# The first norm's token factor applied to the in-projection's sums in PSUM, with x loaded and begun in two token halves

## The chip, the cores and the metric

The kernel runs on one core of a Trainium2 chip. The metric is the device time of one execution in microseconds (us). TensorE (PE) does the matmuls, VectorE (DVE), ScalarE (ACT) and GpSimd (POOL) the rest; SyncE (SP) issues most transfers. The profile names weight loads of TensorE apart (PEld).

## The reference, cut to what matters

The program is a recurrent block followed by a second block. Only the front of the first block meets the change: a norm over the 1024 channels of each of 1024 tokens, the in-projection, and then two branches, a gated recurrence (LRU) and a short convolution (SC).

```python
def rms_norm(x, g):
    xf = x.astype(jnp.float32)
    y = xf * lax.rsqrt(jnp.mean(xf * xf, axis=-1, keepdims=True) + EPS)
    return (y * g.astype(jnp.float32)).astype(x.dtype)
...
        h = rms_norm(x, norm1_g[l])
        z = jnp.einsum('bsd,de->bse', h, w_in[l])
        lru_x, lru_gate, sc_b, sc_c, sc_x = jnp.split(z, splits, axis=-1)
        lru_x = causal_dwconv(lru_x, lru_conv_w[l]) + lru_conv_b[l]
        y_lru = rg_lru(lru_x, lru_wa[l], lru_ba[l], lru_wx[l], lru_bx[l], lru_lambda[l]) \
            * jax.nn.gelu(lru_gate)
        y_sc = sc_b * causal_dwconv(sc_c * sc_x, sc_conv_w[l])
```

The norm is x times a gain per channel times a factor per token. The factor per token can be taken out of the sum over channels, so z can be had as (x times gain) times w_in, times the factor.

## The kernel before

All data is fp32. Activations are held with channels on the 128 partitions and the 1024 tokens along the free axis, so x, which arrives with tokens on partitions (`x_tok`, 4 transfers of 1 MB), is transposed on TensorE: 8 token tiles of 8 transposes each, copied from PSUM into `xs`. A product of full precision is made of three matmuls in fp32r: both operands are split into a rounded part (`_hi`, a cast on ScalarE) and the rest (`_lo`, a subtraction: for weights on GpSimd, for `h` half on VectorE, half on GpSimd). `matmul3` issues the three, each in two halves of 512 tokens; `project` does that for the 8 channel tiles, 48 matmuls for one block of 128 outputs and all 1024 tokens, and then raises `block_done`.

The order on every engine is written out by hand; engines meet at semaphores. There are four PSUM tiles `ps[0]` to `ps[3]` of 1024 columns.

Start (`L603` to `L656`, `L1067` to `L1089`, `L1609` to `L1666`, `L2279` to `L2340`): x is loaded and transposed; VectorE squares 7 token tiles, ScalarE one; the root and its reciprocal give `rstd`, which 8 small matmuls (16 records, L2279) spread over the partitions into `ps[2]`. VectorE then forms h = xs times gain times factor for each channel tile (L1609) into `scr`, ScalarE casts it (L1061), VectorE and GpSimd make the rests (L1621, L958), and `first_two` multiplies the first two blocks, X(0) and G(0), channel tile by channel tile as they come. While TensorE is at that, ScalarE takes one Exp (L1089) and VectorE works out the gates' constants from it in a chain of small steps (L1649 to L1666). The first convolution (`conv_first`, L1098) waits for those constants, for `x_parked` (a 4 MB copy of `xs` to HBM, since the convolution overwrites `xs`) and for X(0).

The recurrence goes over 8 channel tiles c. TensorE's order in it is X(c), the gates of tile c-1 (12 matmuls), G(c). X(c) may begin when `conv_done` says that the convolution of X(c-1) has left `ps[0]`; the gates of c-1 wait for `xc_lo_done`; G(c) waits for `gelu_done` of c-1, which reads `ps[1]`. ScalarE's order is `conv_first(c)`, the cast of the next weights, five curves of tile c-1 (`gate_curves`, with two table loads), a cast of the gate weights, then `gate_gelu(c)`: cast of weights, cast of `xc`, GELU of G(c). VectorE's order is the three taps of the convolution (`convolve(c)`, L1625), `recur(c-1)` (L1680 to L1694, nine steps and among them a scan), `second_parts(c)` (L1698, L1701), and again from the start.

Then come 12 blocks for the SC branch, S(0) to S(11), where ScalarE copies the C part out of PSUM (`sc_c`, L1258), VectorE multiplies it with the X part (L1805), convolves, and multiplies with the B part (L1810). From L2352 on follow the out-projection, the feed-forward part and the second block, which the change doesn't touch but for numbers of a semaphore.

## Time and profile before

| | |
|---|---|
| three runs | 1728.16, 1730.13 and 1732.98 us, median 1730.13 us |
| profiled execution | span of 1726.5 us from the first to the last instruction; no other time of it is on record |
| median of the runs less that span | 3.6 us |
| TensorE matmul busy | 1681.0 us (97%) |
| VectorE busy | 1225.3 us (71%) |
| ScalarE busy | 792.4 us (46%) |
| GpSimd busy | 516.6 us (30%) |
| mean granted TensorE clock | 0.992 of full speed |

The shares are means over stages with different limits. The 3.6 us lie around the span (launch and end). Times in the rows below count from the first instruction of the profiled execution.

### The profile page before, as it was taken

The numbers are of one execution on the slowest core, as the hardware profiler recorded it, in microseconds if no ns is written. First come the engines' busy times: TensorE is split into PE (matmuls) and PEld (weight loads), VectorE is DVE, ScalarE is ACT, GpSimd is POOL, SyncE is SP. The second block draws the span as 40 slices with busy tenths as digits, with TensorE's granted clock in tenths as the row PEclk, the third lists the DMA queues.
The fourth block names the chain that finished last, engine by engine and source line by source line (L and its number), as shares of the span: only waits on it lengthen the run. The fifth ranks groups of instructions, "written<-read, shape, count | busy, mean of one in ns | idle before, by whom it ended". The sixth has DMA issues, their size and how long they took to land.

```text
span 1726.5 us, 20915 instructions
## 1 busy us (share of the span) xinstructions
PE 1681.0 (97%) x7556; PEld 1383.3 (80%) x7556; DVE 1225.3 (71%) x1442; ACT 792.4 (46%) x1038; POOL 516.6 (30%) x284
## 2 busy tenths in 40 slices
PE   7999999999999999999999999998999999999998
PEld 6888878888877888888888888886878877777776
DVE  6577772259999888888888789885636365666554
ACT  5466541235764434343434455553322146676531
POOL 4221222200015555554552000003432242345320
PEclk8999999999999999999999999999999999999999
DMA  8111112152422232222223876651321320110251
GB/s 259 49 36 49 40 45 74 37 201 80 152 81 76 83 97 73 84 84 87 73 86 125 317 237 199 219 159 43 122 74 61 85 86 25 37 49 25 102 215 73
DMA packets 161095, 176.96 MB, mean 102 GB/s; under 512 B 13566, under 2 KB 114692, under 8 KB 161028
## 3 DMA queue, kind: packets, MB, share of 16 engines
q1 hardware_dynamic: 158724, 167.67, 30.3%
q10 hardware_dynamic: 2304, 8.39, 1.3%
q8 instruction: 42, 0.69, 0.2%
q14 instruction: 25, 0.20, 0.0%
HBM read 140.38 MB, written 35.65 MB: 102 GB/s over the span
## 4 chain that ended last, share of the span: by engine, by line
PE 82%; DVE 10%; ACT 4%; issue 1%; POOL 1%; DMA 1%; POOLq 0%; DVEq 0%; ACTq 0%; SPq 0%
PE ps L921 28%; PE ps L2398 24%; PE ps L2352 18%; PE ps L2618 4%; PE ps L2603 3%; PE ps L2648 2%; PE ps L2588 1%; DVE lat L2109 1%; PE ps L2576 1%; DVE pt_lo L2203 1%; DVE prob L2185 1%; POOL z_lo L1015 1%; PE ps L2279 1%; DVE square_dve L1636 0%; ACT pt_hi L1548 0%
## 5 line engine op out<-in xcount | busy, mean ns | idle before, releaser
L945 POOL TENSOR_TENSOR w_lo<-w_raw,w_hi 128x1024 fp32r<-128x1024 f32 x52 | 135.8, 2614 | 623.0 <-ACT w_hi L1044 623.0
L2398 PE MATMUL ps<-hop_hi_P,wop_hi_P 128*128 128x512 f32 x672 | 262.5, 391 | 4.7 <-DVE u L1853 3.3
L2398 PE MATMUL ps<-hop_hi_P,wop_lo_P 128*128 128x512 f32 x672 | 261.5, 389 | 0.0
L2398 PE MATMUL ps<-hop_lo_P,wop_hi_P 128*128 128x512 f32 x672 | 261.5, 389 | 0.0
L921 PE MATMUL ps<-h_hi,w_hi 128*128 128x512 f32 x752 | 235.1, 394 | 11.3 <-DVE h_lo L1621 7.8
L951 POOL TENSOR_TENSOR wop_lo_P<-pair_sum,wop_hi_P 128x512 fp32r<-128x512 f32 x90 | 135.9, 1510 | 354.5 <-ACT wop_hi_P L1055 354.5
L921 PE MATMUL ps<-h_lo,w_hi 128*128 128x512 f32 x752 | 232.9, 391 | 0.0
L921 PE MATMUL ps<-h_hi,w_lo 128*128 128x512 f32 x752 | 232.7, 391 | 0.0
L921 PEld LDWEIGHTS ps<-h_hi,w_hi 128*128 128x128 f32 x752 | 141.4, 189 | 43.3 <-issue 14.0
L921 PEld LDWEIGHTS ps<-h_lo,w_hi 128*128 128x128 f32 x752 | 142.1, 189 | 29.8
L921 PEld LDWEIGHTS ps<-h_hi,w_lo 128*128 128x128 f32 x752 | 142.0, 189 | 29.7
L2398 PEld LDWEIGHTS ps<-hop_hi_P,wop_hi_P 128*128 128x128 f32 x672 | 126.1, 188 | 33.7 <-DVE u L1853 4.5
L2398 PEld LDWEIGHTS ps<-hop_hi_P,wop_lo_P 128*128 128x128 f32 x672 | 126.1, 188 | 26.3
L2398 PEld LDWEIGHTS ps<-hop_lo_P,wop_hi_P 128*128 128x128 f32 x672 | 126.1, 188 | 25.8
L2352 PE MATMUL ps<-dn_x_hi,dn_w_hi 128*128 128x512 f32 x336 | 131.0, 390 | 0.4 <-DVE dn_x_lo L1735 0.4
L2352 PE MATMUL ps<-dn_x_lo,dn_w_hi 128*128 128x512 f32 x336 | 130.7, 389 | 0.0
L2352 PE MATMUL ps<-dn_x_hi,dn_w_lo 128*128 128x512 f32 x336 | 130.7, 389 | 0.0
L1044 ACT CAST w_hi<-w_raw 128x1024 fp32r<-128x1024 f32 x52 | 54.3, 1048 | 130.6 <-PE ps L921 130.0
L1055 ACT CAST wop_hi_P<-pair_sum 128x512 fp32r<-128x512 f32 x96 | 58.8, 614 | 114.9 <-DVE pair_sum L1842 114.8
L951 POOL TENSOR_TENSOR wop_lo_P<-pair_raw,wop_hi_P 128x512 fp32r<-128x512 f32 x67 | 98.5, 1479 | 2.4 <-ACT wop_hi_P L1055 2.2
L1022 POOL TENSOR_SCALAR mask<-pos_f,vec 128x1024 f32<-128x1024 f32 x16 | 67.4, 4211 | 86.3 <-DVE stat L2185 78.1
L2352 PEld LDWEIGHTS ps<-dn_x_hi,dn_w_hi 128*128 128x128 f32 x336 | 63.1, 188 | 14.4 <-DVE dn_x_lo L1735 1.2
(350 smaller groups left out, 3337.9 us busy)
## 6 DMA issues: line engine op xcount, KB each, us to landing
pair_raw<-in_w_up SPq DMA_DIRECT2D x48, 512.0 KB, 4.6
w_raw<-in_w_in SPq DMA_DIRECT2D x46, 512.0 KB, 3.9
dn_raw<-gu_park SPq DMA_DIRECT2D x84, 256.0 KB, 3.9
dn_raw<-in_w_down SPq DMA_DIRECT2D x60, 256.0 KB, 3.1
gu_park<-up_cv SPq DMA_DIRECT2D x24, 512.0 KB, 2.6
out_raw<-in_w_out SPq DMA_DIRECT2D x30, 256.0 KB, 3.0
x_tok<-in_x SPq DMA_DIRECT2D x4, 1024.0 KB, 8.2
x_park<-xs SPq DMA_DIRECT2D x1, 4096.0 KB, 14.3
```

What stands on the lines that cost most here:

```text
L921: mm = nc.tensor.matmul(out_ap[:, t], w, x[:, t], start=a, stop=b)
L945: nc.gpsimd.tensor_tensor(lo[:, :], raw[:, :], hi[:, :].bitcast(f32), ALU.subtract).then_inc(w_lo_done, 1)
L951: nc.gpsimd.tensor_tensor(wop_lo[q][:, :, :], weight_part(q, pair), wop_hi[q][:, :, :].bitcast(f32), ALU.subtract).then_inc(wop_lo_done, 1)
L1015: nc.gpsimd.tensor_tensor(z_lo[e][:, k, :], raw, z_hi[e][:, k, :].bitcast(f32), ALU.subtract).then_inc(zp_lo_done, 1)
L1022: nc.gpsimd.tensor_scalar(mask[1][:, :], pos_f[:, :], vec[:, V_POS + u % NT:V_POS + u % NT + 1], MASKED, ALU.is_gt, ALU.mult).then_inc(mas ...
L1044: nc.scalar.copy(hi[:, :], raw[:, :]).then_inc(w_hi_done, 1)
L1055: nc.scalar.copy(wop_hi[q][:, :, :], weight_part(q, pair)).then_inc(wop_hi_done, 1)
L2352: mm = nc.tensor.matmul(dst, a[:, w], x[:, :], start=first, stop=last, skip_group_check=True)
L2398: mm = nc.tensor.matmul(dst, w[q][:, k, :], x[q][:, k, :], start=a, stop=b, skip_group_check=True)
L2603: mm = nc.tensor.matmul(dst, a[:, k, d], b[:, k, :], start=first, stop=last)
L2618: mm = nc.tensor.matmul(ps[t % 4][:, c], a[e][:, k, cols_t], b[e][:, k, c], start=first, stop=last)
L2648: mm = nc.tensor.transpose(ps[2][:, k * P:(k + 1) * P], prob[w % 3][:, k * P:(k + 1) * P], ident[:, :])
```

## The change

1. Loads. The 16 small row loads (norm gains, convolution weights, constants, positions) go from SP's queue to ScalarE's, at the head of ScalarE's program. SP issues x in the order x0, x1, weights of X(0), x2, weights of G(0), x3.
2. The front in two token halves T1 and T2 (512 tokens each). The copies of the transposes out of PSUM are divided between ScalarE (even tiles) and VectorE (odd). h without the token factor is made per channel tile and half: its rounded part by one ACTIVATE with the gain as scale (`first_high`), its rest by one VectorE instruction (`first_low`). GpSimd makes no rest of h in the first norm. TensorE does X(0) and G(0) on T1 with the transposes of tokens 4 to 7 set among them, then on T2, with the spreading of the factor in it.
3. The factor. ScalarE copies the spread factor from PSUM to `rstd1` in SBUF. VectorE multiplies each X(c) and each G(c) in place in PSUM with it (`by_token_factor`), before `conv_first` and before the GELU. In the SC branch VectorE takes over the C part, multiplied with the factor squared, and multiplies the convolved product with the factor once more.
4. `gelu_gate`, `square_dve` and `rstd1` get other places in SBUF.

```diff
-            def norm(i, gain, dst, rb, lo_before):
+            def by_token_factor(n, c, bank, done):
+                dve.wait_ge(block_done, read(n, c))
+                V.tensor_tensor(bank[:, :], bank[:, :], rstd1[:, :], ALU.mult).then_inc(done, 1)
...
             def convolve(c, one):
                 xc = xs[:, one, :].rearrange("p o t -> p (o t)")
+                by_token_factor(N_LRU, c, ps[0], zx_done)
                 dve.wait_ge(conv_base, c + 1)
...
+            dve.wait_ge(rstd1_spread, 1)
             convolve(0, first)
             second_parts(0, first)
+            by_token_factor(N_LRU + 1, 0, ps[1], zg_done)
             with step.of(11).loop(LRU_TILES - 2) as i:
                 c = i + 1
                 convolve(c, bass.ds(c, 1))
                 recur(i, bass.ds(i, 1))
                 second_parts(c, bass.ds(c, 1))
+                by_token_factor(N_LRU + 1, c, ps[1], zg_done)
             c = LRU_TILES - 1
             convolve(c, last)
             second_parts(c, last)
             recur(c - 1, slice(c - 1, c))
+            by_token_factor(N_LRU + 1, c, ps[1], zg_done)
             recur(c, last)
...
             def conv_first(c, one):
-                act.wait_ge(block_done, read(N_LRU, c))
+                act.wait_ge(zx_done, c + 1)
...
+                act.wait_ge(zg_done, c + 1)
                 gelu = gelu_last if one is last else gelu_gate
```

ScalarE's new order at the start:

```diff
+            xt_copy(0)
+            xt_copy(2)
+            act.wait_ge(vec_t, 1)
+            nc.scalar.copy(vec[:, :], ps[0][:, 0:V_COLS]).then_inc(vec_done, 1)
+            high(0)
...
+            first_high(0, T1)
+            first_high(1, T1)
+            high(1)
+            first_high(2, T1)
+            first_high(3, T1)
+            xt_copy(4)
+            for c in range(4, KT):
+                first_high(c, T1)
+            xt_copy(6)
...
+            for n in range(5, NT):
...
+                token_square(n)
...
+            for c in range(4):
+                first_high(c, T2)
...
+            for c in range(4, KT):
+                first_high(c, T2)
+            act.wait_ge(rb_done, 1)
+            nc.scalar.copy(rstd1[:, :], ps[2][:, :]).then_inc(rstd1_spread, 1)
             act.wait_ge(setup_done, LAM_ABS)
             nc.scalar.activation(small[:, 24:32], small[:, 16:24], ACT.Exp).then_inc(vec_done, 1)
```

VectorE's, and TensorE's:

```diff
+            def first_low(c, t):
+                dve.wait_ge(first_hi, (0 if t is T1 else KT) + c + 1)
+                V.scalar_tensor_tensor(out=h_lo[:, c, t], in0=xs[:, c, t], scalar=col(V_NORM1 + c),
+                                       in1=h_hi[:, c, t].bitcast(f32), op0=ALU.mult, op1=ALU.subtract
+                                       ).then_inc(first_lo, 1)
...
+            xt_copy(3)
+            token_square(2)
+            dve.wait_ge(vec_done, VEC)
+            first_low(0, T1)
+            first_low(1, T1)
+            xt_copy(5)
+            first_low(2, T1)
+            token_square(3)
+            first_low(3, T1)
+            first_low(4, T1)
+            xt_copy(7)
+            first_low(5, T1)
+            token_square(4)
+            first_low(6, T1)
+            first_low(7, T1)
...
+            transposed(4)
+            transposed(5)
+            for k in range(8 + 3):
+                for b, j in ((0, k), (1, k - 3)):
+                    if 0 <= j < 8:
...
+                        first_step(b, j, T1)
+                if k in (3, 4):
+                    transposed(k + 3)
+            for b in range(2):
+                for k in range(8):
+                    first_step(b, k, T2)
+                    if b == 0 and k == 3:
+                        pe.wait_ge(rstd_done, 1)
+                        pe.wait_ge(xt_by_act, 4)
+                        spread(ps[2]).then_inc(rb_done, 1)
```

And in the SC branch:

```diff
-                nc.scalar.copy(scr[0][:, :], ps[n % 4][:, :]).then_inc(sc_c, 1)
+                V.tensor_tensor(scr[0][:, :], ps[n % 4][:, :], rstd1_squared[:, :], ALU.mult).then_inc(sc_c, 1)
...
                 step(tap(scr[2], scr[1], 2, V_SCW + j))
+                step(V.tensor_tensor(scr[2][:, :], scr[2][:, :], rstd1[:, :], ALU.mult))
```

## Rows read from the trace of the kernel before

**Rows 1.** The chain that ended last: start us, us, what.

```profile
26.82 182.38 PE ps L921 x792
...
248.76 109.08 PE ps L921 x480
```

**Rows 2.** Timeline of the start: start us, us, engine, line, what.

```profile
5.96 9.79 PE L2292 MATMUL ps<-ident,x_tok 128*128 128x128 f32 x64 [5.96 <-DMA x_tok<-in_x]
...
11.35 3.79 ACT L1067 COPY xs<-ps 128x1024 f32<-128x1024 f32 x4 [0.69 <-PE ps L2292]
...
19.05 3.78 PE L2279 MATMUL ps<-ident,rstd 128*128 128x128 f32 x16
...
20.92 4.67 POOL L945 TENSOR_TENSOR w_lo<-w_raw,w_hi 128x1024 fp32r<-128x1024 f32 x2 [17.00 <-ACT w_hi L1044]
...
37.23 1.28 ACT L1089 ACT_TABLE_LOAD   x1
...
39.74 0.21 ACT L1089 ACTIVATE small<-small 128x8 f32<-128x8 f32 x1 [1.23 <-DVE half_ba L1651]
...
42.92 0.17 DVE L1666 TENSOR_SCALAR kx<-kh 128x8 f32<-128x8 f32 x1
```

**Rows 3.** Busy time by stretch: PE, PEld, DVE, ACT, POOL; granted clock, DMA share, GB/s.

```profile
11.30:15.80 4.50, 4.46 (x41) 4.22 (x39) 3.55 (x6) 4.45 (x5) 0.00 (x0) 1.00 1.09 288
18.20:22.90 4.70, 4.57 (x20) 4.14 (x20) 0.00 (x0) 3.58 (x5) 1.98 (x1) 0.50 1.06 268
26.80:31.70 4.90, 4.88 (x12) 3.83 (x13) 4.90 (x5) 2.37 (x3) 3.64 (x2) 0.50 1.02 364
31.70:51.00 19.30, 19.30 (x86) 15.80 (x84) 14.62 (x28) 7.89 (x9) 8.11 (x4) 1.00 0.21 58
```

**Rows 4.** Timeline of TensorE where X(1) begins.

```profile
51.15 0.72 PE L921 MATMUL ps<-h_hi,w_hi 128*128 128x512 f32 x2
```

**Rows 5.** Timeline of VectorE and ScalarE over one turn of the loop.

```profile
108.89 1.23 DVE L1701 TENSOR_TENSOR xc_lo<-xs,xc_hi 128x1024 fp32r<-128x1024 f32 x1
...
111.52 1.21 ACT L1098 ACTIVATE xs<-ps,vec 128x1024 f32 x1 [2.04 <-PE ps L921]
...
113.00 1.28 DVE L1625 SCALAR_TENSOR_TENSOR xs<-ps,vec,xs 128x1023 f32 x1 [2.88 <-ACT xs L1098]
...
119.40 0.69 DVE L1680 TENSOR_SCALAR scr<-scr 128x1024 f32<-128x1024 f32 x1 [2.17 <-ACT scr L1118]
...
127.27 4.37 DVE L1692 TENSOR_TENSOR_SCAN xs<-scr,root 128x1024 f32 x1
...
133.38 1.22 DVE L1701 TENSOR_TENSOR xc_lo<-xs,xc_hi 128x1024 fp32r<-128x1024 f32 x1
...
136.00 1.21 ACT L1098 ACTIVATE xs<-ps,vec 128x1024 f32 x1 [2.04 <-PE ps L921]
```

**Rows 6.** Timeline of GpSimd in that turn.

```profile
113.74 2.41 POOL L945 TENSOR_TENSOR w_lo<-w_raw,w_hi 128x1024 fp32r<-128x1024 f32 x1 [8.73 <-ACT w_hi L1044]
126.11 3.39 POOL L945 TENSOR_TENSOR w_lo<-w_raw,w_hi 128x1024 fp32r<-128x1024 f32 x1 [9.96 <-ACT w_hi L1044]
```

**Rows 7.** Groups by line and form: count, busy us, mean ns, idle before.

```profile
L1928 DVE TENSOR_TENSOR ps<-ps,xs 128x1024 f32<-128x1024 f32 x48 | 59.2, 1232 | 1.6
L1237 ACT ACTIVATE xs<-x_early,vec 128x512 f32<-128x512 f32 x8 | 5.3, 714 | 2.3 <-DVE x_early L1786 2.3
L2069 DVE COPY scr<-ps 128x1024 f32<-128x1024 f32 x4 | 4.9, 1224 | 28.2 <-PE ps L921 28.2
L1735 DVE TENSOR_TENSOR out_x_lo<-xs,out_x_hi 128x512 fp32r<-128x512 f32 x34 | 23.5, 692 | 0.0
L1692 DVE TENSOR_TENSOR_SCAN xs<-scr,root 128x1024 f32<-128x1024 f32 x2 | 4.6, 2292 | 0.1
```

**Rows 8.** Waits of TensorE, 209 to 360 us: total, times, longest.

```profile
PE ps L921 <- POOL w_lo L945: 1.5, 1, 1.5
```

**Rows 9.** DMA issues: KB, median us to landing.

```profile
x_park<-xs SPq DMA_DIRECT2D x1, 4096.0 KB, 14.3
```

More of the change, by code:

```diff
@@ L203, in program @@
         root = tile("root", G0, 14)
-        gelu_gate = tile("gelu_gate", G0, 15)
+        gelu_gate = tile("gelu_gate", G0, 0)
+        rstd1 = tile("rstd1", G0, 15)
         gelu_last = tile("gelu_last", G0, 8)
-        square_dve = tile("square_dve", G0, 15)
+        square_dve = tile("square_dve", G0, 14)
         pair_raw = [at("pair_raw0", G0 + 8 * TILE, [2, KT, P]), at("pair_raw1", W0, [2, KT, P])]
@@ L1064, in xt_copy @@
             def xt_copy(t):
                 act.wait_ge(xt_done, t + 1)
-                nc.scalar.copy(xs[:, :, t * P:(t + 1) * P], ps[t % 3][:, :].rearrange("p (c q) -> p c q", c=KT)
-                               ).then_inc(xt_copied, 1)
-            for t in range(NT - 2):
-                xt_copy(t)
-            act.wait_ge(x_in[3], 16)
-            nc.scalar.activation(scr[4][:, :], x_tok[:, NT - 1, :], ACT.Square,
-                                 accum_out=small[:, NT - 1:NT]).then_inc(sumsq, 1)
@@ L1076, in _, with first_high, token_square @@
-            act.wait_ge(sumsq, 1)
-            act.wait_ge(sumsq_dve, NT - 1)
+                nc.scalar.copy(xs[:, :, t * P:(t + 1) * P], ps[TOKEN_BANK[t]][:, :].rearrange("p (c q) -> p c q", c=KT)
+                               ).then_inc(xt_by_act, 1)
+            def first_high(c, t):
+                nc.scalar.activation(h_hi[:, c, t], xs[:, c, t], ACT.Identity, scale=col(V_NORM1 + c)).then_inc(first_hi, 1)
+            def token_square(n):
+                nc.scalar.activation(scr[4][:, :], x_tok[:, n, :], ACT.Square,
+                                     accum_out=small[:, n:n + 1]).then_inc(sumsq, 1)
@@ L1630, in _, with token_square @@
                 V.memset(sign[32 * q:32 * q + 32, :], -1.0 if q % 2 == 0 else 1.0).then_inc(setup_done, 1)
-            for n in range(NT - 1):
-                if n % 2 == 0:
-                    dve.wait_ge(x_in[n // 2], 16)
+            def token_square(n):
+                dve.wait_ge(x_in[n // 2], 16)
                 if n >= 1:
@@ L1863, in part_of, with wop_low @@
                 return token_part(name, h)
-            def first_low(q, n):
+            def wop_low(q, n):
                 dve.wait_ge(wop_hi_done, nth(q, Pair(0, n)))
@@ L1902, in _ @@
             half_squares(2)
-            first_low("P2", 1)
+            wop_low("P2", 1)
             half_squares(3)
@@ L1907, in _ @@
             hop_low("P6")
-            first_low("P6", 0)
+            wop_low("P6", 0)
             dve.wait_ge(root_done, 2)
@@ L1912, in _ @@
             hop_low("P7")
-            first_low("P5", 1)
+            wop_low("P5", 1)
             dve.wait_ge(x1_parked[1], 16)
-            first_low("P7", 0)
+            wop_low("P7", 0)
             second_sum(Pair(0, 0))
@@ L1918, in _ @@
             hop_low("P3")
-            first_low("P6", 1)
+            wop_low("P6", 1)
             hop_low("P4")
-            first_low("P4", 0)
+            wop_low("P4", 0)
             def scale(pair, name):
@@ L1973, in period @@
                 if the(k, 0):
-                    first_low("P3", 0)
+                    wop_low("P3", 0)
                     pair_sums(Pair(0, 1), (2, 3))
@@ L2316, in first_two, with first_step @@
                             mm.then_inc(block_done, 1)
-            pe.wait_ge(xt_copied, NT)
-            first_two(0, (ps[0], ps[1]), 0)
+            def first_step(b, k, t):
+                pe.wait_ge(first_lo, (0 if t is T1 else KT) + k + 1)
+                wh, wl = blocked(b)
+                for w, x, first, last in ((wh, h_hi, k == 0, False), (wh, h_lo, False, False), (wl, h_hi, False, k == 7)):
+                    mm = nc.tensor.matmul(ps[b][:, t], w[:, k, :], x[:, k, t], start=first, stop=last)
+                if k == 7 and t is T2:
+                    mm.then_inc(block_done, 1)
+            transposed(4)
[3 more added lines that the diff above has]
+                    if 0 <= j < 8:
+                        if j == 0:
+                            pe.wait_ge(w_lo_done, b + 1)
+                        if j == 0 and b == 0:
+                            pe.wait_ge(vec_done, VEC)
+                        if j == 0 and b == 1:
+                            pe.wait_ge(xt_by_dve, 1)
+                        first_step(b, j, T1)
[8 more added lines that the diff above has]
+                        spread(ps[2]).then_inc(rb_done, 1)
             def gates():
```

176 lines of the change are left out of this document (94 added, 82 removed).

## The prediction

> **What bounds the kernel now.** The shares of busy time say TensorE (97%), but the change touches the first 360 us only, so I read that stretch. The chain of waits comes first: from 26.82 us TensorE's matmuls are the chain without a break, up to the recurrence's end, and again from 248.76 [rows 1]. Ahead of 26.82 stands a front in which TensorE does only transposes (5.96 to 15.75) and the spread [rows 2]. So a microsecond saved before 26.82 is a microsecond saved, if nothing later gives it back. Two more views decide whether something does. The stretches by granted clock: after the transposes TensorE runs at 0.50 (1.2 GHz) up to 31.7 us, then at full clock [rows 3]. And one turn of the recurrence's loop on the other engines [rows 5]: the turn is 136.00 - 111.52 = 24.48 us, which is TensorE's 108 matmuls. Is there a second loop just below it? From the start of `conv_first` (111.52) to the first step of `recur` (119.40) are 7.88 us, in which VectorE depends on ScalarE's curves; from there to the end of the `xc_lo` subtraction (133.38 + 1.22 = 134.60) 15.20 us more. VectorE and ScalarE together need 23.08 us for a turn in which each step waits for the one before; only 1.40 us are free, although VectorE's busy share doesn't show it. That is the number on which the prediction rests.
>
> **The change, part by part: the loop.** It puts two multiplies in place in PSUM on VectorE into each turn. The same form (PSUM tile of 1024 columns by an SBUF tile, back into PSUM) takes 1.232 us in this kernel [rows 7], no more and no less to be expected; with some 0.07 for each handover, 2.6 us in all. The one on X(c) stands ahead of `conv_first`, so ScalarE's curves and `recur` move back by it; the one on G(c) stands between `xc_lo` and the next turn's first instruction, and ScalarE's GELU behind it. Neither lies beside a wait. The turn of VectorE and ScalarE becomes 23.08 + 2.6 = 25.7 us, against TensorE's 24.48: TensorE waits 1.2 us a turn, for `xc_lo_done`. Of the turns the first costs 0.4 (it uses up the 1.40 that are free, and its `recur` starts without one before it), the next five 1.2 each: 6.4 us.
>
> That turn holds one stall already: the scan takes 4.37 us in the loop and 2.29 outside it, while GpSimd makes the rest of the next weights (126.11, 3.39 us); GpSimd's other one, at 113.74, takes 2.41 and lies beside VectorE's taps, which read PSUM and don't stretch (1.28) [rows 5, 6, 7]. So two streams from SBUF on VectorE and a GpSimd subtraction exclude each other, and one with an operand in PSUM doesn't take part. The multiplies have one operand in PSUM and stay out of it; the stall stays at one a turn.
>
> **The recurrence's end.** VectorE: taps of tile 7, `second_parts`, `recur(6)`, multiply of G(7), `recur(7)`. The GELU of G(7), which had run under `recur(6)`, now comes after it, and ScalarE's last curves behind the GELU. Then come the casts of the weights of S(2), for whose rest TensorE already waits 1.5 us [rows 8]. To that chain are added 1.3 (X multiply), 1.3 (G multiply), 1.0 (GELU, of the size of a 1024-column copy, 3.79 / 4 = 0.95 [rows 2]), and taken from it 0.9 (the copy of the C part, now VectorE's): 2.7 us. It also starts late by the 1.2 us for which the multiply of X(7) queues behind that of G(6). S(2) comes 3.9 us later against X(7): as two waits, S(1) for the GELU and S(2) for its weights. It is 3 us if GpSimd's stalls fall better here, 5 if worse; I take 3.6, since part of TensorE's wait lies under the loop's own. Loop and end: 10 us, from 8 to 12.
>
> **The SC branch.** VectorE gets three more operations for each j and ScalarE one less. A group of three blocks takes TensorE 33 us and VectorE's steps for it are some 10; `sc_c` of j = 0 comes after `recur(7)`, but S(4), which waits for it, begins two blocks (22 us) after S(2). I cost it at nothing; cover gone, it would be 1.2 us once.
>
> **The start.** What the change takes away is real: no multiply by the factor before the first matmul, no wait for all of x. Tokens 0 to 3 are transposed by about 12.1 us (64 transposes in 9.79, the first at half the pace [rows 2]), the small rows' transposes come at about 13, `vec` 13.3, the cast of the first weights (1.0) 14.3, GpSimd's rest of them (4.67 / 2 = 2.3) 16.7, `first_low(0)` 17.8 with the exclusion above: it reads `xs` and `h_hi` from SBUF and has to wait for GpSimd. First matmul at 17.8, 9.0 us before that of [rows 1]. But from there the halves are fed by long queues:
>
> - T1. `first_low(1)` meets GpSimd's second rest, 20.8. TensorE's matmuls run at 1.2 GHz (0.43 us each in 26.80:31.70, 0.227 at full clock [rows 3]), since the clock fell after the transposes here and nothing else precedes them there. VectorE does a copy (1.22), a square, lows of 0.69 [rows 7]; its copy of token tile 7 waits for the transposes of that tile, which TensorE makes only after step k = 4, at half clock: k = 3 for both blocks 24.6 to 27.3, tile 6 to 28.6, k = 4 to 30.6, tile 7 to 31.6. `first_low(5)` stands behind the copy: 33.5. The last five steps end at 40.4.
> - T2. 48 matmuls of 0.227 = 10.9 and the spread, half of 3.78 at full clock: 53.2. X(0) is complete at 47.7.
> - The chain behind it. The spread ends at 45.0 and only then does ScalarE copy `rstd1` (1.0), load the Exp table (1.28) and take the Exp (0.21); before, table and Exp were done at 39.95, under the first matmuls. VectorE's chain of constants from there takes 42.92 + 0.17 - 39.95 = 3.1 us [rows 2]: 50.6. The multiply of X(0) stands in VectorE's queue behind it (1.3), then `conv_first` (1.2) and three taps (113.00 to 117.2, 4.2) before X(1) may begin: 57.4, against 51.15 [rows 4, 5].
>
> So the start ends 6.2 us later, not 9 earlier. `x_parked` is also wanted by `conv_first(0)`: it is issued after the copy of tile 7, 32.8 + 14.3 [rows 9] = 47.1, hidden by 3.5 us. The 16 row loads at the head of ScalarE's queue take some 6 us there, in which it has nothing to copy yet: the first tile's transposes end at 7.7. ACTIVATE with a scale, 512 columns, takes 0.714 [rows 7]; ScalarE is not last.
>
> Bounds of the start: at full clock from the first matmul on, T1 ends 2.5 us earlier: +3.7. At half clock up to 36 us: +7.8. Row loads late by 5 us: +1.5 more. If the two first lows did not wait for GpSimd: 1.8 less.
>
> The Trainium skill (SBUF - State Buffer, section "SBUF: two separate sides") has the exclusion as an exclusive lock of a port pair that a VectorE instruction with two SBUF inputs and a GpSimd one hold for a whole instruction; the trace agrees (4.37 against 2.29), and by the rule the first two lows wait, which is the 1.8 us above. The Trainium skill (TensorE: Matmul & The Clock Gate, "Part 4: PE-mode transpose") says that transposes do not count as work for the clock. The trace agrees: 4.46 of 4.50 us busy with transposes, and 0.50 granted after them. By that rule the first matmuls of the change find the low clock; without it the result is 2.5 us less.
>
> **The sum.** Start +6.2, loop +6.4, end +3.6: 16.2 us on the profiled span of 1726.5, which the median of the runs exceeds by 3.6. 1730.1 + 16.2 = 1746.3; I say 1746.
>
> **Rivals.**
> - The start comes even (0.20): X(1) within 2.5 us of before, since the clock rises early or the feeding overlaps better than my queue by queue sum. For it: the bounds above; against it: Exp and constants stand behind the spread in any case. Loop and end stay: 1730 + 10 = 1740 (1737 to 1743).
> - Faster (0.04): the 1.40 us of free time are more than I read, VectorE's recurrence absorbs both multiplies, and the 9 us of the first matmul reach X(1) less the 3 that the last chain adds: 1724. It decides at a turn of VectorE and ScalarE below 24.48; I have 25.7.
> - The loop hides the multiplies, the start is late as forecast (0.06): only start and some of the end, +7: 1737.
> - The low clock stays for most of the front, or rows and weights land late (0.09): T1 and T2 both slow, +20 to +25: 1752.
> - The forecast (0.61): 1743 to 1750.
>
> **How the numbers follow.** A measurement of this kernel tells about 0.3% (5.2 us) from no change. Forecast, the even start, the slow front and most of the third are slower by more than that: 0.92; half of the third and a little of the second are same: 0.04; faster 0.04. The range reaches from 1737 (even start with the loop's low bound) to 1752; it leaves out the faster case, a part of the slow front and of the third.
>
> **What the profile after would show.** First matmul of X(0) near 18 us, with gaps before the first five k. Copy of `rstd1` behind the spread, table load, Exp, constants on a chain up to X(1) near 57. In the loop a turn of 25.7 us on all engines, TensorE waiting 1.2 us for `xc_lo`, no wait of VectorE for X's matmuls. VectorE's multiplies 1.23. Waits at S(1) and S(2). From S(2) on the same lengths as before. It is wrong if turns stay at 24.5, or if X(1) begins before 49.

## The result

The changed kernel takes 1758.58 us (median of 4 runs, 1755.07 to 1760.85), the kernel before beside it 1730.56 us. The ratio is 1.0156, with a 95% interval from 1.0136 to 1.0176: slower by some 28 us. The forecast was 1746, with a range from 1737 to 1752. The direction and the places of the loss were as forecast, the size was not.

The profiled execution has a span of 1756.3 us against 1726.5, a difference of 29.8 us where the medians differ by 28.0. The changed kernel's profiled execution took 1758.27 us, 2.0 more than its span, so the 3.6 us that the kernel before has above its span are not all launch and end: about 1.6 of them (an estimate from these two numbers) are that it was profiled in one of its faster executions. Four marks of the same kind in both traces cut the difference: the first matmul of X(1), the starts of `conv_first(1)` and `conv_first(7)`, and the first matmul of the out-projection. The forecast is put into the same cuts: of its 3.6 for the end, the 1.3 us of the multiply ahead of `conv_first` belong to the second cut here.

| stretch | before | after | measured | forecast |
|---|---|---|---|---|
| up to X(1) | 51.15 | 60.00 | +8.85 | +6.2 |
| X(1) to `conv_first(1)` | 11.42 | 14.06 | +2.64 | +1.3 |
| six turns, to `conv_first(7)` | 146.65 | 159.05 | +12.40 | +6.4 |
| from there to the out-projection | 148.46 | 151.25 | +2.79 | +2.3 |
| out-projection to the last instruction | 1368.8 | 1371.9 | +3.1 | 0 |
| sum | 1726.5 | 1756.3 | +29.8 | +16.2 |

**The chain of the changed kernel**, the stretch that answers to [rows 1] (start us, us, what):

```profile
6.91 7.57 DMA freq<-in_rope_freq
14.64 2.33 DVE xs L1670 x2
18.12 1.94 DVE h_lo L1676
20.80 2.86 DVE h_lo L1676
...
60.00 12.54 PE ps L906 x48
...
113.78 3.32 DVE root L1753
118.38 2.30 DVE xs L1755
123.69 3.07 PE ps L906 x12
...
262.90 121.62 PE ps L906 x528
```

In [rows 1] TensorE was the chain without a break from 26.82 to 209 us. Now the chain begins with a transfer of small rows, and in each turn it goes through VectorE and ScalarE and comes back to TensorE for the twelve matmuls of the gates. Only from 262.90 on is TensorE the bound again. The row at 60.00 shows one thing more: 48 matmuls take 12.54 us there, against 48 times 0.227 = 10.9, because TensorE was granted 0.50 from 59.5 to 62.9 us, at the end of an idle time of 4.07 us.

**The timeline of the start**, which answers to [rows 2, 4]:

```profile
14.50 0.21 DVE L1683 CAST pos_rows<-pos_rows_i 8x128 f32<-8x128 int32 x1 [5.92 <-DMA freq<-in_rope_freq]
...
21.02 0.47 PE L2397 MATMUL ps<-h_hi,w_hi 128*128 128x512 f32 x1 [2.16 <-DVE h_lo L1676]
...
36.33 0.50 PE L2397 MATMUL ps<-h_hi,w_hi 128*128 128x512 f32 x1 [1.98 <-DVE h_lo L1676]
...
45.79 1.95 PE L2350 MATMUL ps<-ident,rstd 128*128 128x128 f32 x16
...
48.81 1.28 ACT L1123 ACT_TABLE_LOAD   x1
...
53.35 1.23 DVE L1729 TENSOR_TENSOR ps<-ps,rstd 128x1024 f32<-128x1024 f32 x1
...
60.00 1.21 PE L906 MATMUL ps<-h_hi,w_hi 128*128 128x512 f32 x2 [4.07 <-DVE xs L1651]
```

The first number in brackets is the idle time before the instruction. Read from below: X(1) waits 4.07 us for the taps, these for the multiply at 53.35, this for the constants, these for the table at 48.81, and that for the spread. Read from above: VectorE stands still for 5.92 us until the small rows have landed, because the cast of `pos_rows` is ahead of its copies of tiles 1 and 3.

**One turn of the loop**, which answers to [rows 5]:

```profile
100.56 1.20 ACT L1132 ACTIVATE xs<-ps,vec 128x1024 f32 x1
...
108.43 0.69 DVE L1743 TENSOR_SCALAR scr<-scr 128x1024 f32<-128x1024 f32 x1 [2.18 <-ACT scr L1152]
...
113.78 3.31 DVE L1753 TENSOR_TENSOR root<-scr,root 128x1024 f32<-128x1024 f32 x1
117.12 1.22 DVE L1754 TENSOR_TENSOR root<-root,scr 128x1024 f32<-128x1024 f32 x1
118.38 2.29 DVE L1755 TENSOR_TENSOR_SCAN xs<-scr,root 128x1024 f32 x1
...
122.41 1.23 DVE L1764 TENSOR_TENSOR xc_lo<-xs,xc_hi 128x1024 fp32r<-128x1024 f32 x1
123.55 2.35 DVE L1729 TENSOR_TENSOR ps<-ps,rstd 128x1024 f32<-128x1024 f32 x2
...
124.85 1.28 ACT L1174 ACT_TABLE_LOAD   x1 [10.77 <-DVE ps L1729]
126.15 1.02 ACT L1174 ACTIVATE gelu_gate<-ps 128x1024 f32<-128x1024 f32 x1
127.07 1.20 ACT L1132 ACTIVATE xs<-ps,vec 128x1024 f32 x1
```

From `conv_first` to `conv_first` it is 127.07 - 100.56 = 26.51 us; the forecast had 25.7. The two multiplies end at 125.9, but `conv_first` begins 1.2 us later, since it stands behind the GELU, and the GELU behind a table load that starts only when the multiply of G is done. Before, that load lay in the idle time ahead of the wait, as the timeline of ScalarE in the kernel before shows:

```profile
127.00 1.28 ACT L1139 ACT_TABLE_LOAD   x1
132.94 1.03 ACT L1139 ACTIVATE gelu_gate<-ps 128x1024 f32<-128x1024 f32 x1 [4.65 <-DVE xs L1694]
```

TensorE waits twice in such a turn: 0.84 us for `xc_lo` (at 123.69), where the forecast had 1.2, and 0.56 us for the GELU (at 127.30), which the forecast didn't have.

The stall of the turn is there once, as forecast: it fell on the product with `root` now (3.31 against 1.22 for the same form in the next row), and the scan takes 2.29 instead of the 4.37 of [rows 5].

### The profile page after: what moved, and what is told of

The parts are those of the page before. It is cut to its first block, busy times and chain, and to the rows that moved or that the text cites. A ratio compares the mean times of both kernels' runs of the same rounds, so it can differ in the third digit from the quotient of the medians.

```text
span 1756.3 us, 20965 instructions
## 1 busy us (share of the span) xinstructions
PE 1695.1 (97%) x7556; PEld 1388.4 (79%) x7556; DVE 1256.6 (72%) x1471; ACT 789.3 (45%) x1043; POOL 503.1 (29%) x280
## 4 chain that ended last, share of the span: by engine, by line
PE 74%; DVE 15%; ACT 5%; issue 3%; DMA 1%; POOL 1%; ACTq 0%; POOLq 0%; DVEq 0%; SPq 0%
PE ps L2499 24%; PE ps L906 19%; PE ps L2453 17%; PE ps L2719 4%; PE ps L2704 3%; PE ps L2749 1%; PE ps L2689 1%; DVE root L1753 1%; DVE xs L1755 1%; DVE lat L2180 1%; PE ps L2397 1%; PE ps L2677 1%; DVE root L1754 1%; DVE pt_lo L2274 1%; DVE prob L2256 1%
## 5 line engine op out<-in xcount | busy, mean ns | idle before, releaser
L930 POOL TENSOR_TENSOR w_lo<-w_raw,w_hi 128x1024 fp32r<-128x1024 f32 x52 | 131.9, 2538 | 666.6 <-ACT w_hi L1028 666.6
L906 PE MATMUL ps<-h_hi,w_hi 128*128 128x512 f32 x720 | 226.2, 395 | 16.5 <-DVE xs L1651 4.1
L906 PE MATMUL ps<-h_lo,w_hi 128*128 128x512 f32 x720 | 223.2, 391 | 0.0
L906 PE MATMUL ps<-h_hi,w_lo 128*128 128x512 f32 x720 | 223.2, 391 | 0.0
L906 PEld LDWEIGHTS ps<-h_hi,w_hi 128*128 128x128 f32 x720 | 135.4, 190 | 49.1 <-issue 13.4
L906 PEld LDWEIGHTS ps<-h_lo,w_hi 128*128 128x128 f32 x720 | 136.1, 189 | 28.8
L906 PEld LDWEIGHTS ps<-h_hi,w_lo 128*128 128x128 f32 x720 | 136.0, 189 | 28.6
L2499 PEld LDWEIGHTS ps<-hop_hi_P,wop_lo_P 128*128 128x128 f32 x672 | 126.7, 189 | 26.7
```

Source lines behind the costliest of these rows:

```text
L906: mm = nc.tensor.matmul(out_ap[:, t], w, x[:, t], start=a, stop=b)
L930: nc.gpsimd.tensor_tensor(lo[:, :], raw[:, :], hi[:, :].bitcast(f32), ALU.subtract).then_inc(w_lo_done, 1)
L2499: mm = nc.tensor.matmul(dst, w[q][:, k, :], x[q][:, k, :], start=a, stop=b, skip_group_check=True)
```

## The experiments

### The loop

**1. One wait ahead of the GELU.**

```diff
-                if one is last:
-                    act.wait_ge(xc_lo_done, c + 1)
-                elif one is not first:
-                    act.wait_ge(y_done, c)
                 act.wait_ge(zg_done, c + 1)
```

> The changed kernel, with one edit on ScalarE: the GELU waits for the multiply of G alone. Its other wait (for y, in the last tile for the low part of xc) is left out; VectorE does that work ahead of the multiply of G in its own queue, so it adds no order. Theory (the table load is held back by the second wait): the load of 1.28 us for the GELU runs ahead of the wait again, the GELU ends 1.28 us earlier, and the convolution's first tap with it until the multiply of X (ended 1.1 to 1.2 us after the multiply of G) takes over as the last thing awaited: the turn goes from 26.5 to 25.4 us, six turns and the end make some 7 to 8 us less than the changed kernel, 1750 to 1751 us. Rival A (the load's place has another cause, or the turn is set by the sum of VectorE's work): turn 26.5 us, same time as the changed kernel.

Measured: 1752.49 us, ratio 1.0115 [1.0079, 1.0151]; profiled span 1749.9. ScalarE's timeline:

```profile
113.03 1.28 ACT L1170 ACT_TABLE_LOAD   x1
123.71 1.03 ACT L1170 ACTIVATE gelu_gate<-ps 128x1024 f32<-128x1024 f32 x1 [9.40 <-DVE ps L1725]
125.07 1.21 ACT L1132 ACTIVATE xs<-ps,vec 128x1024 f32 x1 [0.33 <-DVE ps L1725]
```

The load is back at the head of the idle time, and the turn is 125.07 - 99.46 = 25.61 us. The forecast of this run had 25.4. TensorE's wait for the GELU is gone, that for `xc_lo` is left (0.82). The out-projection begins at 376.57 against 384.36, 7.8 us earlier: 5.6 over the six turns, and 2.0 behind them, where TensorE's wait for the last GELU (`gelu_last`) ahead of S(1) falls to 1.60 us. In the changed kernel it is 3.05:

```profile
262.90 0.73 PE L906 MATMUL ps<-h_hi,w_hi 128*128 128x512 f32 x2 [3.05 <-ACT gelu_last L1174]
```

The table load behind the second wait is 0.9 us of each turn, and the rest of the turn is what the forecast said. This rests on the marks of the two traces. The times of the runs say less: `one_wait`'s four lie between 1745.04 and 1754.78 us, and its interval overlaps that of the changed kernel.

**2. Without one of the multiplies, and without both.** `no_g` takes out the multiply of G and the wait for it, `no_x` that of X (`conv_first` waits for `block_done` again), `no_xg` both. What they leave out is the token factor in those sums.

```diff
-            by_token_factor(N_LRU + 1, 0, ps[1], zg_done)
...
-                by_token_factor(N_LRU + 1, c, ps[1], zg_done)
...
-                by_token_factor(N_LRU, c, ps[0], zx_done)
```

The first lines go in `no_g` and `no_xg`, the last in `no_x` and `no_xg`.

> The changed kernel without the multiply of G: the token factor is left out of G's sums and the GELU no longer waits for it. Theory (the turn is a cycle through VectorE and ScalarE with 1.40 us of room over TensorE's 24.48): one multiply of 1.23 us fits in the room, and the table load goes back ahead of the wait, so the turn is TensorE's 24.5 us; six turns and the end give back 14 to 17 us, 1742 to 1745 us. Rival A (every microsecond on VectorE is paid): turn 26.5 - 1.3 = 25.2 us, 8 to 9 us back, 1750 us. Rival B (the loop isn't where the time went): under 3 us back.

> The changed kernel without the multiply of X: the token factor is left out of X's sums, and the first tap waits for the block itself. Theory (the cycle runs multiply of G, table load, GELU, first tap, and the multiply of X lies beside the load and the GELU): only VectorE's queue gets shorter by 1.23 us while the first tap still stands behind the GELU; X's multiply is off the cycle, so the turn stays within 0.2 us of 26.5 and the time within 2 us of the changed kernel, but for 1.3 us at the first tile (no multiply of X ahead of the first tap there), about 1756 us. Rival A (every microsecond on VectorE is paid alike): turn 25.2, 1749 us.

> The changed kernel without both multiplies: what is left is the new front (x in two token halves, the first blocks early) and the small gates. The token factor is left out of X and G. Theory (loop and front add up): the loop's turn is TensorE's 24.5 us as in the kernel before; left are the late start of X(1) (60.0 less the first tile's multiply, some 58.7, against 51.15) and an end of the phase like that before: 1730.1 + 7.5 = 1737 to 1740 us. Rival (the front costs nothing, all is in the loop): 1730 to 1732 us. Rival (the loop is slower for another reason, say the low clock): 1745 us or more.

Measured, with the mean turn over the six turns:

| | time us | ratio [95%] | X(1) | mean turn | out-projection |
|---|---|---|---|---|---|
| changed kernel | 1758.58 | 1.0156 [1.0136, 1.0176] | 60.00 | 26.51 | 384.36 |
| no_g | 1743.67 | 1.0075 [1.0048, 1.0102] | 59.32 | 24.70 | 369.01 |
| no_x | 1754.51 | 1.0140 [1.0115, 1.0166] | 57.97 | 26.51 | 381.04 |
| no_xg | 1737.03 | 1.0035 [1.0022, 1.0049] | 58.55 | 24.44 | 365.44 |
| before | 1730.73 | | 51.15 | 24.44 | 357.68 |

The two multiplies last the same 1.23 us and are worth quite different amounts. Without G's, 1.8 us a turn are gone; without X's, nothing. The timelines of VectorE and ScalarE in `no_x` show why:

```profile
120.50 1.23 DVE L1729 TENSOR_TENSOR ps<-ps,rstd 128x1024 f32<-128x1024 f32 x1
...
125.49 1.28 DVE L1651 SCALAR_TENSOR_TENSOR xs<-ps,vec,xs 128x1023 f32 x1 [3.77 <-ACT xs L1132]
```

```profile
121.80 1.28 ACT L1174 ACT_TABLE_LOAD   x1 [10.78 <-DVE ps L1729]
123.10 1.02 ACT L1174 ACTIVATE gelu_gate<-ps 128x1024 f32<-128x1024 f32 x1
124.02 1.20 ACT L1132 ACTIVATE xs<-ps,vec 128x1024 f32 x1
```

VectorE has 1.23 us less to do and idles 3.77 us instead of 2.63. The cycle is multiply of G, load, GELU, `conv_first`, and X's multiply lies beside the load. `no_g` has a single wait before the GELU, so it gets both back, the multiply and the load. Its turns alternate between 24.5 and 25.0 us instead of staying at TensorE's 24.48; why is not shown.

**3. The old front with the new loop.** Both multiplies go into the kernel before, by a tile of ones, with the changed kernel's waits.

> The kernel before, with its own front, and with both multiplies put into the loop (by a tile of ones, so that the sums stay as they are) and the GELU behind two waits, as in the changed kernel. Theory (front and loop add up, the loop is some three quarters of the loss): X(1) begins at 51.15 us as before, the turn is 26.5 us as in the changed kernel, the output projection begins 8 to 9 us earlier than the changed kernel's 384.36, at 375 to 377 us; 1748 to 1751 us. Rival (the loop is slow only behind the new front, say by the new places of the gates or the order of the loads): turn 24.5 to 25 us and under 1738 us.

Measured: 1751.65 us, ratio 1.0131 [1.0109, 1.0152]. X(1) begins at 50.78, the turn is 26.51, the out-projection begins at 374.53. So 374.53 - 357.68 = 16.9 us are the loop's and its end's, and 365.44 - 357.68 = 7.8 us (`no_xg`) the front's: 24.6 of the 26.7 us that the changed kernel has lost at the out-projection. Of the 2.1 us that are left, 1.8 lie ahead of X(1): 60.00 - 51.15 = 8.85, against 58.55 - 51.15 = 7.40 and 50.78 - 51.15 = -0.37. Part of that is no effect of an edit, since X(1) begins at 50.78 in this run and at 52.65 in `old_front_xg_late` (below), whose start is the same.

**4. The stall moved.**

```diff
                 low(N_LRU + 2, c)
+                pool.wait_ge(xc_lo_done, c + 1)
                 low(N_LRU + 3, c)
```

> The changed kernel with one edit on GpSimd: the second subtraction for the weights of a turn waits for xc_lo, so that it lies beside the two multiplies, which have an operand in PSUM, instead of beside VectorE's product with root, which takes 3.31 us there against 1.22 for the same form next to it. Theory (a GpSimd subtraction and a two-operand VectorE instruction from SBUF exclude each other, and one with a PSUM operand is free of it): the product takes 1.2 us, the multiplies stay at 1.2, VectorE's and ScalarE's turn falls from 26.51 by 2.1 us to below TensorE's 24.48, and the turn is 24.5 us; about 12 us less than the changed kernel, 1745 to 1748 us. Rival A (the multiplies are stretched instead, by the same 2.1 us): turn stays 26.5 us. Rival B (the weights' low part now comes too late for G, 2.4 us behind xc_lo against TensorE's 2.7 us of gates): TensorE waits for w_lo and the turn is 25 us or more.

Measured: 1741.61 us, ratio 1.0068 [1.0049, 1.0086], 17 us less than the changed kernel, of which 12.2 are there at the out-projection, which begins at 372.20 (for the others see "After the out-projection"), and 3.4 less than the lowest time forecast for this run. The turn is 24.48. VectorE:

```profile
111.88 1.23 DVE L1754 TENSOR_TENSOR root<-scr,root 128x1024 f32<-128x1024 f32 x1
...
119.57 1.22 DVE L1730 TENSOR_TENSOR ps<-ps,rstd 128x1024 f32<-128x1024 f32 x1
121.62 1.23 DVE L1730 TENSOR_TENSOR ps<-ps,rstd 128x1024 f32<-128x1024 f32 x1 [0.83 <-PE ps L906]
```

GpSimd in the same time:

```profile
119.80 2.39 POOL L930 TENSOR_TENSOR w_lo<-w_raw,w_hi 128x1024 fp32r<-128x1024 f32 x1 [16.54 <-DVE xc_lo L1765]
```

The subtraction lies beside both multiplies and stretches neither; the product with `root` is back at 1.23. Idle time of VectorE is now 0.83 us ahead of the multiply of X, and its releaser is TensorE: the turn is TensorE's again, with both multiplies in it, and the table load still behind the second wait. The 2.1 us of the stall are worth more than the multiplies' excess over the free time. The Trainium skill (SBUF - State Buffer, "SBUF: two separate sides") states the exclusive lock between GpSimd and a VectorE instruction with two inputs from SBUF; the runs here agree with it: the product and the scan, with both inputs in SBUF, are stretched (3.31 and 4.37 us against 1.23 and 2.29), the multiplies, with one in PSUM, are not (1.22 and 1.23).

Is that also so behind the old front, and does the kernel before gain from it without the multiplies?

> The kernel before with both multiplies in its loop (by ones), and GpSimd's second subtraction behind xc_lo. Theory (with the exclusion moved away the two multiplies fit in the loop): X(1) at 51 us, turn 24.5 us, only the end of the recurrence is longer, by 2 to 4 us: 1731 to 1735 us. Rival (the loop gains from the edit only behind the new front): over 1740 us.

> The kernel before with one edit: GpSimd's second subtraction of a turn behind xc_lo. Theory (before, TensorE sets the turn, and VectorE's stall of 2.1 us lies in its slack): the scan falls from 4.4 to 2.3 us, the turn stays at 24.48, and the time is the same within 2 us. Rival (each stall costs): 6 turns of 2.1 us, 1718 us. Rival (without the multiplies the subtraction falls on another two-operand instruction, or TensorE waits for w_lo): slower by up to 5 us.

Measured: 1737.86 us, ratio 1.0042 [1.0030, 1.0054], for the first; its turn is 24.48, from X(1) (52.65) to the out-projection (364.09) it takes 311.4 us against 306.5 in the kernel before. That was longer than expected (1731 to 1735 us): the multiplies cost nothing in the loop, but 4.9 us at its two ends, 1.3 between X(1) and `conv_first(1)` and 3.4 behind `conv_first(7)`. For the second: 1728.03 us, ratio 0.9989 [0.9980, 0.9998], a difference that is hardly one. Its scan takes 2.29 us instead of 4.37, and VectorE then idles 4.96 us before the first tap instead of 2.88 [rows 5]:

```profile
125.91 2.29 DVE L1693 TENSOR_TENSOR_SCAN xs<-scr,root 128x1024 f32 x1
...
136.13 1.28 DVE L1626 SCALAR_TENSOR_TENSOR xs<-ps,vec,xs 128x1023 f32 x1 [4.96 <-ACT xs L1099]
```

The same stall costs nothing where TensorE sets the turn and 2 us a turn where VectorE and ScalarE do.

### The start

**5. Constants ahead of the spread.** `mended` is the changed kernel with edits 1 and 4, and the Exp and the chain of constants moved up:

```diff
             for c in range(4, KT):
                 first_high(c, T1)
+            act.wait_ge(setup_done, LAM_ABS)
+            nc.scalar.activation(small[:, 24:32], small[:, 16:24], ACT.Exp).then_inc(vec_done, 1)
             xt_copy(6)
...
             dve.wait_ge(vec_done, VEC)
+            step(V.scalar_tensor_tensor(out=small[:, 16:24], in0=vec[:, V_LAM:V_LAM + 8], scalar=-1.0,
+                                        in1=vec[:, V_LAM:V_LAM + 8], op0=ALU.mult, op1=ALU.min))
+            V.tensor_scalar(half_ba[:, :], vec[:, V_BA:V_BA + 8], 0.5, None, ALU.mult).then_inc(setup_done, 1)
...
             first_low(0, T1)
...
             first_low(4, T1)
...
+            V.tensor_scalar(kx[:, :], kh[:, :], -2.0, None, ALU.mult).then_inc(setup_done, 1)
             xt_copy(7)
```

> The changed kernel with three edits: the GELU behind one wait, GpSimd's second subtraction behind xc_lo, and the Exp with the chain of constants moved from behind the spread into VectorE's and ScalarE's idle time at token tile 6 and 7. Theory: the first multiply of X no longer waits for the constants, X(1) begins when G(0) ends (55.9 us instead of 60.0), TensorE's idle 4.1 us there is gone, the turn is 24.5 us, and the two waits at the end shrink. The output projection begins at 364 to 367 us against 384.4 and 357.7 before; 1737 to 1741 us, still slower than before by what the first matmuls at the low clock and the feed of the two halves cost. Rival A (moving the constants into the feed delays the lows by their 3 us, and G(0) ends as much later): X(1) at 58 to 59, 1741 to 1744. Rival B (the new front is as good as the old once the constants are away): X(1) by 52, 1733.

Measured: 1738.11 us, ratio 1.0054 [1.0034, 1.0074]. X(1) begins at 56.87, 3.1 us earlier and 1.0 later than the forecast of that run; the out-projection begins at 365.50, as forecast. The forecast took X(1) to begin when G(0) ends. G(0) ended by then (55.56 against 55.93 in the changed kernel), but X(1) waits 1.31 us more, for the taps:

```profile
50.23 1.23 DVE L1726 TENSOR_TENSOR ps<-ps,rstd 128x1024 f32<-128x1024 f32 x1 [7.59 <-PE ps L2394]
...
52.82 3.92 DVE L1648 SCALAR_TENSOR_TENSOR xs<-ps,vec,xs 128x1023 f32<-128x1023 f32 x3 [1.36 <-ACT xs L1133]
...
56.87 0.73 PE L906 MATMUL ps<-h_hi,w_hi 128*128 128x512 f32 x2 [1.31 <-DVE xs L1648]
```

From the end of X(0) the multiply, `conv_first` and three taps take longer than the 24 matmuls of G(0) that are left. The wait is 1.31 us in `feed` too, and 1.32 in the kernel before with both multiplies (`old_front_xg`). It is a price of the multiply of X(0) that no order of the front took away.

The edit also did something that it was not meant to do. VectorE and GpSimd at 17 us:

```profile
17.87 2.30 DVE L1685 SCALAR_TENSOR_TENSOR small<-vec 128x8 f32<-128x8 f32 x1
20.21 2.28 DVE L1687 TENSOR_SCALAR half_ba<-vec 128x8 f32<-128x8 f32 x1
22.40 0.16 DVE L1688 TENSOR_SCALAR half_bx<-vec 128x8 f32<-128x8 f32 x1
```

```profile
16.88 5.57 POOL L930 TENSOR_TENSOR w_lo<-w_raw,w_hi 128x1024 fp32r<-128x1024 f32 x2 [12.96 <-ACT w_hi L1029]
```

Instructions of 8 columns, 0.16 us elsewhere, take 2.3 us each: they wait out GpSimd's subtractions. The first matmul moved from 21.02 to 23.70 by my own edit. It did no harm at the end of G(0), which came 0.4 us earlier all the same.

**6. The feed.** `feed` is `mended` with another order of the same instructions. VectorE: copies of tiles 1 and 3, cast of `pos_rows`, square 2, low 0, copy of tile 5, lows 1 to 3, copy of tile 7, the small instructions on `vec`, low 4, the constants, low 5, squares 3 and 4, and on as before. ScalarE copies tile 6 after `first_high(4)`. TensorE:

```diff
-                if k in (3, 4):
-                    transposed(k + 3)
+                if k in (0, 1):
+                    transposed(k + 6)
```

> The kernel mended with another order of the front's work: VectorE's cast of pos_rows behind the copies of tiles 1 and 3 (it waited there for the small rows from 8.5 to 14.3 us), the copy of tile 5 between the first two lows, no constants beside GpSimd's first weights, and token tiles 6 and 7 transposed after steps 0 and 1 instead of 3 and 4. Theory (what makes the start late is the feed: the small rows at 14.5 us, the lows that meet GpSimd's subtractions, tile 7 in the middle of T1): the first matmul is near 20.5 us, the idle of 2 us before step 5 is gone, and X(1) begins at 53.5 to 55 us instead of 56.87; 1735 to 1737 us. Rival (TensorE's own 96 matmuls with their stretch at half clock set G(0)'s end, whatever the feed): X(1) within 0.7 us of mended.

Measured: 1737.19 us, ratio 1.0039 [1.0026, 1.0052]. First matmul at 19.74, X(1) at 53.49, 3.4 us before that of `mended` and 6.5 before the changed kernel's; the out-projection begins at 362.14. The rival, X(1) within 0.7 us of `mended`, is out. But one part of the theory is out as well: the idle time ahead of step k = 5 isn't gone (TensorE waits for lows 1.93 us before 31.22 and 1.54 before 34.40). And the clock moved with the order: from its first matmul on, `mended` was at 0.50 up to 28.4 and again from 35.2 to 38.6, `feed` from 20.3 to 23.7 alone. The order brings the first matmul 4.0 us forward; how much of the 3.4 us is the clock's is not separated. X(1) is still 2.3 us later than the 51.15 of the kernel before, and 1.31 of them are the wait for the taps. The time gained against `mended`, 0.9 us in the medians, is less than the 3.4 at the mark. The two profiled executions differ by 3.35 us up to 380 us and by 0.3 at the end; the gain goes where both share the code, as described below under "After the out-projection".

**7. The clock.** Extra matmuls that nothing uses, in the gaps of TensorE ahead of the first block.

```diff
+            for i in range(8):
+                nc.tensor.matmul(ps[0][:, 0:P], ident[:, :], ident[:, :], start=True, stop=True)
             pe.wait_ge(rows_in, 16 * 16)
```

> The kernel mended, with eight extra matmuls of 128 columns (ident by ident, into ps0, overwritten later) before the small rows' transposes and eight before the first block, where TensorE has nothing else to do. They compute nothing that is used. Theory (TensorE stands at 1.2 GHz at its first matmuls because it did transposes and waited before them, and T1 is long because of it): with matmuls in the gaps the clock stays up for more of 15 to 32 us; at 0.23 instead of 0.43 us each the first half ends 2 to 4 us earlier, X(1) with it, 1734 to 1738 us. Rival (VectorE and the token tiles feed T1, and the clock hides behind it): the clock is high, the matmuls take 0.23 us, and waits between them grow: X(1) within 1 us of mended. Rival (sixteen matmuls are too few): clock and times as in mended.

> The kernel before with extra matmuls of 128 columns that nothing uses: twelve between the transposes and the small rows, eighteen behind the spread. Theory (the stretch at 0.50 from 18.2 to 31.8 us comes from a TensorE that only transposed and waited): part of it is at full clock, the spread takes 1.9 instead of 3.8 us and the first matmuls 0.23 instead of 0.43; 2 to 4 us less, 1726 to 1728 us. Rival (as in mended_warm, other engines set the pace, and the clock's gain is small): the same within 1 us. Rival (at half clock the extra matmuls take 3 to 4 us and delay the spread): slower by 1 to 3 us.

Measured: 1738.46 us, 1.0056 [1.0036, 1.0075], and 1729.36 us, 0.9995 [0.9984, 1.0006]. Both are the kernel without them within what can be told. In `mended_warm` the clock was at full speed up to 22.1 us instead of in part of that, and low again from there to 28.9, when TensorE had waited 3.92 us for the first low; X(1) came at 57.13 instead of 56.87. In `before_warm` it did what it was meant to do; the stretches of [rows 3], in the nearest bounds (columns as there):

```profile
18.20:22.90 4.70, 4.70 (x44) 4.60 (x43) 2.00 (x2) 3.43 (x5) 2.65 (x2) 1.00 1.10 284
26.20:31.70 5.50, 4.63 (x18) 3.17 (x18) 5.50 (x5) 3.01 (x3) 4.21 (x2) 1.00 1.02 363
```

The granted clock is 1.00 where it was 0.50, but TensorE is busy for 4.63 of 5.50 us instead of 4.88 of 4.90: it now waits for the rests of h. X(1) begins at 49.98, 1.2 us earlier. That is not shown to be the extra matmuls' doing. In `before_late`, whose start is that of the kernel before without any edit, the clock was 1.00 up to 22.9 and 0.50 only from there to 29.8, and X(1) began at 49.77. So one execution and another of the same start differ by as much. The low clock at the start was cheap, since the feeding engines were just behind. The Trainium skill (TensorE: Matmul & The Clock Gate, "Part 4: PE-mode transpose") says that transposes don't count as work for the clock; the two kernels differ in nothing but matmuls behind the transposes, and agree with it. They don't prove it: the extra matmuls also fill idle time, and the runs don't tell transposes from idle time.

### After the out-projection

The table of the result has 3.1 us there, in a part of the kernel that both share. Busy time and clock of the changed kernel in one stretch of it, where the kernel before was granted 1.00:

```profile
520.30:527.10 6.80, 6.80 (x21) 5.64 (x21) 4.83 (x8) 5.08 (x7) 0.00 (x0) 0.50 0.00 0
```

The twelve matmuls of 512 columns in it take 5.27 us, from 521.48 to 526.75; the same twelve take 2.86 us in the kernel before (494.23 to 497.09). Up to here the trace of the changed kernel lies 26.7 us behind the other (517.58 against 490.90), right after it 29.8 us (528.87 against 499.04), and 29.8 at the end. So the 3.1 us of the table arise in this one stretch. In `late_w_lo`, `before_late` and `before_warm` such stretches lie in other places, or are missing (none near 500 us in `late_w_lo`). One and the same kernel shows it too: of 13 runs of the kernel before, seven took 1727.92 to 1730.73 us at a mean clock of 0.992, six 1732.27 to 1734.40 us at 0.986 to 0.988. So such microseconds come and go without any change. Whether the change makes them more frequent is not shown, and what places the stretches stays open.

## Why the prediction was right or wrong

- **The start, +8.85 against +6.2.** The chain behind the spread was right to a tenth: from the end of the spread (47.7) to X(1) are 12.3 us, as forecast (45.0 to 57.4, 12.4), with table load, Exp, constants, multiply, `conv_first` and taps in the forecast order. What failed is "first matmul at 17.8": it came at 21.02. The forecast had the small rows' transposes "at about 13"; the rows landed at 14.48, and VectorE had the cast that waits for them ahead of two copies and a square, which the forecast left out of its queue. With the cast behind the copies (`feed`) the first matmul comes at 19.74, although the rows are as late, so 1.3 of the 3.2 us are the order's. The rest is late rows and GpSimd's first subtractions, 2.8 and 3.5 us long instead of 2.3. T1 ended 2.65 us late (43.05 against 40.4), and all behind it. The bound "row loads late by 5 us: +1.5 more" was too small for the same reason. That the first lows meet GpSimd's subtractions was right, and that `x_parked` is hidden (issued at 35.70, 13.0 us to landing, against `conv_first` at 54.70).
- **X(1), +1.3 more than forecast.** The wait of 4.07 us was in the sum; that the clock falls in it, so that X(1) takes 12.54 us, was not.
- **The loop, +12.4 against +6.4.** The step that failed is "the turn of VectorE and ScalarE becomes 23.08 + 2.6 = 25.7". The multiplies took 1.23, the stall stayed at one a turn, and TensorE waits for `xc_lo`, all as forecast. The step put the GELU's table load, 1.28 us, at nothing: [rows 5] don't hold it, since it had lain in idle time (127.00, shown above). Behind the multiply of G it lies on the path, and TensorE waits for the GELU too. With it out of the way the turn is 25.61 (experiment 1) and the six turns cost 153.44 - 146.65 = 6.8 us. The forecast let the first turn cost only 0.4 us; it cost as much as the others, 1.1 (25.60). The number on which the prediction rested, 23.08, stands.
- **The end, +2.79 against +2.3.** The size came out near by luck. With the table load out of the way (`one_wait`) the same stretch is 376.57 - 227.30 = 149.27 us, only 0.8 more than before, where the sum has 2.3; the load adds the other 2.0. Nor are the waits those of the forecast. It had one at S(1) for the GELU and one at S(2) for its weights. The changed kernel has 1.43 us ahead of the gates of tile 7, for `xc_lo`, 3.05 us at S(1), and none at S(2), where the kernel before waits 1.5 [rows 8]. Why the multiplies cost less there than the sum has is open. That the SC branch costs nothing was right.
- **The rest, +3.1,** lies in one stretch of low clock, in code that the change doesn't touch; the forecast had nothing there.
- **The range.** Its upper end took up late rows and a low clock, but each cost was bounded as if the work on ScalarE kept its place. Of the 10.5 us by which the sum up to the out-projection is off (26.7 against 16.2), 7.6 are the table load's (159.05 - 153.44 = 5.6 in the turns, 2.0 at the end), 2.65 the feed's, 1.3 lie at X(1) and 0.4 in the rest of the turns; the end without the load takes 1.5 back.
- **The rivals.** "The start comes even" needed X(1) by 53.65: `feed` just gets there (53.49), the changed kernel doesn't. "The loop hides the multiplies" fell for the change as it was made, but it is what one wait on GpSimd gives: 24.48 with both in it.

No version with the token factor in PSUM beats the kernel before. The best, `feed`, is 1.0039 [1.0026, 1.0052]: its X(1) is 2.3 us later, and from X(1) to the out-projection it takes 308.65 us instead of 306.53.

## What to carry to other kernels

When work is put on the free time of a loop, write down the cycle with each engine's instructions in it, those that lie in idle time too: a table load of 1.28 us that costs nothing ahead of a wait cost 0.9 us a turn behind one. A multiply's price is not its length but its place; two of 1.23 us cost 1.8 us a turn and nothing. And before a loop is called full, look for an instruction that takes longer in it than elsewhere: moving the neighbour that it meets gave more (2.0 us a turn, 26.51 to 24.48) than taking out either multiply (1.8 and nothing).

## What the runs showed of the hardware that was not expected

- ScalarE's table load ran ahead of the wait of its ACTIVATE when that had one wait (`one_wait`, `no_g`, and the kernel before) and behind it when it had two (the changed kernel, `no_x`, `late_w_lo`). The load takes 1.28 us and the ACTIVATE starts 1.30 us after it. The Trainium skill (ScalarE: Activation LUTs, "What ACT_TABLE_LOAD costs") has 1283 ns for it, which agrees, and 1380 ns of drain beside it for every switch. That differs from the rows here: no drain shows on the path.
- The exclusion between GpSimd and VectorE is not a matter of size: instructions of 8 columns took 2.30 and 2.28 us beside GpSimd's subtraction of 1024 columns, against 0.16 alone. The second, a `TENSOR_SCALAR`, reads one tile only, so the stall isn't confined to instructions with two streams from SBUF, as the prediction has it.
- TensorE's clock fell to 0.50 at an idle time of 4.07 us in the middle of full work (from 59.5 us) and behind one of 3.05 us (from 264.3 us); in `no_x` at one of 2.93 us (from 58.0 us). But behind idle times of 3.02 us ahead of the same block S(1) it stayed at 1.00 in `old_front_xg` (252.4 us) and `old_front_xg_late` (242.0 us). Where TensorE idled 1.31 us ahead of X(1) (`mended`, `feed`) it did not fall. So the length of the idle time alone doesn't settle it.
